# First banded attention: the second group of a unit's transposes is issued ahead of the values of the unit before it

## What is computed

```python
def window_gqa(q, k, v, sinks):
    ...
    kb, vb = bands(k), bands(v)          # blocks n-1, n, n+1
    scores = jnp.einsum('bnqhgd,bnkhd->bnhgqk', qb, kb) * (ATTN_HEAD_DIM ** -0.5)
    ...
    mask = (jnp.abs(rel) <= WINDOW)[None] & ((k_abs >= 0) & (k_abs < S))[:, None, :]
    scores = jnp.where(mask[None, :, None, None], scores, NEG)
    m = jnp.maximum(jnp.max(scores, axis=-1, keepdims=True), s)
    p = jnp.exp(scores - m)
    probs = p / (jnp.sum(p, axis=-1, keepdims=True) + jnp.exp(s - m))
    out = jnp.einsum('bnhgqk,bnkhd->bnqhgd', probs, vb)
```

## Time and profile before

| | |
|---|---|
| median of 3 runs | 3047.69 us (3042.49 to 3051.21) |
| the profiled execution's own time | 3045.61 us |
| its span, first to last instruction | 3043.8 us |
| mean granted TensorE clock | 0.992 of full speed |
| the banded attention in it | from 242.66 us (first scores) to 428.13 us (end of the last values) |

### The profile page before, as it was taken

How to read it: one execution, slowest core, us unless ns; L and a number is a source line. 1 busy time by engine, 2 the same in 40 slices (tenths; PEclk the granted TensorE clock), 3 DMA queues, 4 the chain that set the end, 5 groups by cost and what they waited for, 6 DMA issues and landing times.

```text
span 3043.8 us, 35198 instructions
## 1 busy us (share of the span) xinstructions
PE 2956.6 (97%) x13896; PEld 2311.9 (76%) x13896; DVE 2142.7 (70%) x3303; ACT 1243.6 (41%) x2121; POOL 89.9 (3%) x70
## 2 busy tenths in 40 slices
PE   8999989999999999999999999999999999999998
PEld 7885557878888888888877788888888786666666
DVE  7746866687777777689964887777777735566675
ACT  4214642432222222478832522222223516876652
POOL 0003520000000000000000000000000000000000
PEclk9999999999999999999999999999999999999999
DMA  4430024111111111211131011111111131000213
GB/s 155 118 94 8 1 98 140 55 50 51 52 56 49 49 56 56 101 45 46 52 139 42 21 56 56 53 46 56 56 50 61 49 126 34 21 21 22 97 52 114
DMA packets 72804, 190.47 MB, mean 63 GB/s; under 512 B 8320, under 2 KB 8704, under 8 KB 72512
## 3 DMA queue, kind: packets, MB, share of 16 engines
q1 hardware_dynamic: 72640, 188.23, 19.2%
HBM read 172.20 MB, written 14.68 MB: 61 GB/s over the span
## 4 chain that ended last, share of the span: by engine, by line
PE 80%; DVE 10%; ACT 7%; issue 2%; DMA 0%; POOL 0%; SPq 0%; DVEq 0%; ACTq 0%; POOLq 0%
PE PS L1490 42%; PE PS L279 25%; PE PS L366 2%; DVE sm L908 2%; PE PS L320 1%; ACT p L926 1%; PE PS L887 1%; PE PS L873 1%; PE PS L2784 1%; PE PS L2801 1%; PE PS L899 1%; PE PS L2775 1%; PE PS L1092 1%; PE PS L1084 1%; ACT p L233 1%
## 5 line engine op out<-in xcount | busy, mean ns | idle before, releaser
L1490 PE MATMUL PS<-p 128*128 128x512 f32 x5760 | 1318.0, 391 | 13.3 <-DVE p L1401 7.7
L1490 PEld LDWEIGHTS PS<-p 128*128 128x128 f32 x5760 | 1083.0, 188 | 246.6 <-ACT p L1395 8.5
L279 PE MATMUL PS<-p 128*128 128x512 f32 (+1 forms) x4560 | 1057.0, 390 | 26.3 <-DVE p L475 9.6
L279 PEld LDWEIGHTS PS<-p 128*128 128x128 f32 x4560 | 840.5, 189 | 231.5 <-issue 39.8
L1687 DVE TENSOR_TENSOR p<-p,PS 128x512 f32<-128x512 f32 x480 | 327.7, 683 | 64.5 <-PE PS L1490 51.2
L241 DVE TENSOR_TENSOR p<-p 128x1024 fp32r<-128x1024 f32 x138 | 163.7, 1190 | 142.5 <-ACT p L233 142.3
L1299 DVE TENSOR_TENSOR p<-p 128x512 fp32r<-128x512 f32 x224 | 154.2, 688 | 112.3 <-ACT p L1293 111.4
L1627 ACT ACTIVATE p<-p 128x512 fp32r<-128x512 f32 x128 | 80.2, 628 | 346.0 <-DVE p L1676 329.6
L1293 ACT ACTIVATE p<-p 128x512 fp32r<-128x512 f32 x224 | 140.1, 625 | 184.9 <-PE PS L1490 159.5
L233 ACT ACTIVATE p<-p 128x1024 fp32r<-128x1024 f32 x138 | 141.7, 1030 | 172.9 <-PE PS L279 111.5
L926 ACT ACTIVATE p<-PS,sm 128x256 f32<-128x256 f32 (+2 forms) x256 | 127.9, 508 | 173.7 <-DVE sm L914 94.1
(11 more groups left out here) (236 smaller groups left out, 2785.3 us busy)
## 6 DMA issues: line engine op xcount, KB each, us to landing
p<-in_in_dram SPq DMA_DIRECT2D x72, 512.0 KB, 3.5
p<-in_up_dram SPq DMA_DIRECT2D x128, 256.0 KB, 2.6
p<-in_dn_dram SPq DMA_DIRECT2D x128, 256.0 KB, 2.6
p<-in_out_dram SPq DMA_DIRECT2D x42, 512.0 KB, 3.6
p<-in_ada_dram SPq DMA_DIRECT2D x24, 512.0 KB, 3.6
p<-in_x_dram SPq DMA_DIRECT2D x16, 512.0 KB, 8.0
p<-in_kv_dram SPq DMA_DIRECT2D x16, 512.0 KB, 3.5
spill_dram<-p SPq DMA_DIRECT2D x16, 512.0 KB, 3.9
```

What stands on the lines that cost most here:

```text
L279: ins = e.matmul(ps[:, c:c + m], weights(b, j, wi), x[:, c:c + m], start=first and i == 0, stop=end and i == 2)
L1490: ins = e.matmul(PS[:, bank, :], w[:, wi, :], x[:, xi, :], start=start and i == 0, stop=stop and i == 2, skip_group_check=open_)
```

## The change

In `pe_banded0` the call that issues the transposes of `(u-1, j)` is moved ahead of the block that issues the values of `u-2`. For `j` 0 there are no values in the step, so nothing moves there. The instructions, their operands and the work of all other engines stay as they were.

```diff
@@ -986,14 +986,14 @@
                         pe_window_scores(P, e, "b0", hs, j, S, n, kp, half, kbs, Qt, Kt, 4, bias0, None)
+                    if 1 <= u <= 32:
+                        pe_turn(P, e, "b0", u - 1, j, len(UNITS0[u - 1][3]), GROUPS0[j], Pb0, TB0,
+                                [("pn", "b0", hs - 2), ("pq", "b0", hs - 2)], j == 1)
                     if j == 1 and u >= 2:
                         n, kp, half, kbs = UNITS0[u - 2]
                         pe_window_values(P, e, "b0", u - 2, n, kp, half, kbs, 7, PT0, Vt, None)
                         if half == 1:
                             P.held[7] = [("oh", "b0", u - 2), ("ol", "b0", u - 2)]
-                    if 1 <= u <= 32:
-                        pe_turn(P, e, "b0", u - 1, j, len(UNITS0[u - 1][3]), GROUPS0[j], Pb0, TB0,
-                                [("pn", "b0", hs - 2), ("pq", "b0", hs - 2)], j == 1)
```

## The result

The changed kernel takes 3090.31 us (median of 4 runs, 3084.54 to 3092.85) against 3048.03 for the kernel before (also 4 runs); the ratio is 1.0137, with a 95% interval from 1.0119 to 1.0155. That is 42 us slower (36 to 47), where 39 were forecast.

The account below looks back on a forecast made before the run. TensorE, busy 2956.6 of 3043.8 us, was taken as the bound. Losses of 33.0 + 3.7 + 1.3 + 1.1 = 39.1 us gave 3084.7 (profiled execution) or 3086.8 (median); forecast 3085.5, range 3074 to 3102.

Parts of the forecast that it names:

- The values are the cover for POOL's wait: Banded attention: TensorE runs the values while it would otherwise wait for POOL's scaling; both last about 1.5 us.
- Odd unit 6.89, even unit 7.52: Forecast us from a unit's first scores to the next unit's, summed along the waits; a pair 14.41 against 11.66.
- 12 pairs, 33.0 us: Loss forecast for the 12 pairs of units with three key blocks, 2.75 us more per pair.
- First four units, 1.1 us: Pipeline fill: step 2 loses nothing; in step 3 the transposes start no earlier and 1.05 us of values come on top.
- Last four units and the end, 3.7 + 1.3 = 5.0 us: Two pairs with two key blocks lose 1.8 us each; the stage's last values end 1.3 us later.
- Nothing gained by earlier transposes: Earlier copies costed at nothing, since they wait for the values through the single PT0; at most 0.6 us a pair.
- The rival of the clock: TensorE's clock falls to 1.2 GHz: about 3119 us over half the pairs, 3152 over all; chance 0.07.
- the clock at 1.00 from about 260 us on: Sign that the forecast is right: full TensorE clock in the changed profile from about 260 us.
- The other rivals: Smaller loss as stalls go, 3079 us (0.03); no effect as values pass waiting transposes, 3047.7 (0.02); faster, about 3040 (0.01).
- The later stages move as a whole: Stages behind the banded attention start 39 us later, with nothing changed in them.
- its own sum for the median (3086.8): The 39.1 us loss applied to the median of the runs shown, 3047.7 us.
- the places where two and three key blocks meet: Pairs where the chain counts both extra waits as full; reason for saying 3085.5 us rather than 3086.8.

Follow-up runs that it names:

- e1: Kernel before with only the wait for pn and pq moved ahead of the values, instruction order kept: 3076.94 us, ratio 1.0104.
- e3: Kernel after the change with POOL's scaling moved to DVE, which scales both heads: 3058.82 us, ratio 1.0049 to the kernel before.
- e9: Kernel before with POOL's scaling moved to DVE, which scales both heads: 3048.18 us, ratio 1.0015.
- e2: Kernel after the change with two PT0 tiles used in turns: 3085.59 us, ratio 1.0136 to the kernel before.
- e11: Kernel after the change with POOL's scaling split into two instructions of half the columns: 3106.08 us, ratio 1.0200 to the kernel before.

## Why the prediction held, point by point

- *The values are the cover for POOL's wait.* Shown: e1 puts the wait in front of the values, moves no transposes and loses 30 us of stage; e3 and e9 shorten the wait and the move costs 9 instead of 40.
- *Odd unit 6.89, even unit 7.52.* Measured 6.83 and 7.49, a pair of 14.32 for 14.41. TensorE starts 0.14 us behind POOL both times, between the 0.11 and 0.17 of the prediction. What is left of the difference lies in the transposes and the values, 0.78 and 1.45 us from start to start where 0.81 and 1.49 were put in.
- *12 pairs, 33.0 us.* From the first scores of unit 4 to those of unit 28 it is 171.98 us (266.12 to 438.10) against 139.77 (262.61 to 402.38): 32.2. The agreement is partly luck. The dip near 272 us is in it with 1.6. Without it (by the same units in e2) the first of these pairs would lose 1.7 us and not 2.75, as its values still have two key blocks, and the other 11 lose 28.9 together where 30.3 were forecast.
- *First four units, 1.1 us.* Measured 20.86 against 19.95: 0.9.
- *Last four units and the end, 3.7 + 1.3 = 5.0 us.* Measured 34.44 against 27.27 (from the first scores of unit 28 to the first matmul of the next stage): 7.2. This term was too small, for two reasons. The values lag two units behind the scores, so the first of these two pairs still carries values and transposes with three key blocks: 12.86 us (438.10 to 450.96) against 10.14, 2.7 more in place of 1.8. And the clock fell for some 3 us near 457, where a group of transposes took 1.08 us in place of 0.63 and the values 1.98 in place of 1.08: 1.3 us by the same unit of e2.
- *Nothing gained by earlier transposes.* Shown by e2. The reason given, the single `PT0`, was not the one that decides: without it the copies do start earlier, and the maximum behind them waits for the scores anyway.
- *The rival of the clock.* It did not happen on the scale feared: 1.00 in the middle of the stage. But it happened twice for a moment, near 272 and 457 us, for 2.9 us of loss, and in e11, with POOL's scaling 0.26 us longer, for 31 us at the lower clock. The sign "the clock at 1.00 from about 260 us on" did not quite hold. The Trainium skill ("TensorE: Matmul & The Clock Gate", section "A second HAM failure mode: psum-queue depth-cycling") tells of another kernel in which short idle moments between groups of matmuls made the clock swing. The trace of e11 agrees (0.93 over 222 us, the longest idle moment of TensorE in them 1.80 us), that of the changed kernel in its two dips only.
- *The other rivals.* No values passed the waiting transposes: those at 336.40 stand behind the transposes at 335.62. Of TensorE's two short stalls a pair, 0.26 and 0.33 us, the first is gone and the second is still there; the loss is no smaller for it.
- *The later stages move as a whole.* They did, to 0.7 us.

The forecast was 3085.5, 5 us low. Its sum of 39.1 us stands against 40.3 in the stage, and this is closer than the mechanism by itself: without the two dips the stage would have lost 37.4, so the sum was 1.7 us too large, and the clock, which it had at nothing, put 2.9 back. The prediction also went 1.3 us below its own sum for the median (3086.8), to make room for the places where two and three key blocks meet. At the full clock the first such place costs 1.0 us less than the chain says, the second 0.9 more. The remaining 2 us or so between the stage's 40.3 and the 42 of the medians lie outside the stage, where dips of the clock come and go between executions; they are not shown to be the change's.

## What to carry to other kernels

Before an instruction group that waits is moved ahead of one that doesn't, look at what the engine does while the wait runs. If the wait and the second group start together and end together in the trace, the second group is the cover. If the loop also comes back through it, as here, the swap puts most of its length on every round (1.2 and 1.4 us of 1.5 in this case). Such a loss could be worked out here to within 5% by adding differences of starts round the circle of waits, once for each kind of unit. Count the units by the stage of the slowest lagging part (here the values), not by the scores. And while reading such a circle, look for the links in which an in-order engine waits although its next instruction is ready: here a swap of two DVE instructions was worth 8.8 us.

## What the runs showed of the hardware

In these runs the clock of TensorE fell in a stage whose stalls are all short, and a small change made a large difference. With stalls of 1.35 and 1.53 us in each pair, 70.00 of 90 us busy, the granted clock was 1.00 in the middle of the stage. With stalls of 1.61 and 1.79 us (e11) it dipped to 1.2 GHz again and again, each time for some microseconds, 31 us in all. Before the change a stretch at 6.05 of 10 us busy had kept 1.00. These are one profile of each kernel; e2's, with the same unit times as the kernel after, has no dip from 262 us to the end of the stage, so whether one comes also differs between executions or with details that the unit times don't show. A dip also came in a stage that is not touched: the one between 90 and 100 us, worth 1.7 us, is in the profile after and not in the one before.
